# Where the modulation vector of a two-layer decoder trunk is summed: TensorE or VectorE

## The reference, cut to what matters

```
mod = silu(c) @ ada_w[layer] + ada_b[layer]      # 6 x 1024 numbers, one row for all tokens
h   = rms_norm(x, g_mix) * (1 + scale1) + shift1
proj = h @ w_in                                  # 2728 columns: SSD, MLA and MoBA inputs
y   = concat(ssd(...), mla(...), moba(...))      # each normalised
x   = x + gate1 * (y @ w_out)
h   = rms_norm(x, g_ffn) * (1 + scale2) + shift2
x   = x + gate2 * moe(h)                         # 16 experts, 2 of them for each token
```

## Time and profile before

| | us |
|---|---|
| median of 3 runs | 1639.8 (1638.78 to 1642.62) |
| profiled execution: its own time | 1642.98 |
| profiled execution: span, first to last instruction | 1641.2 |
| PE busy in the span | 1447.4 (88%) |
| DVE busy | 981.5 (60%) |
| ACT busy | 699.3 (43%) |
| DMA, mean rate | 226 GB/s |
| mean granted clock of TensorE | 0.930 of full speed |

### The profile page before, as it was taken

One profiled execution on the slowest core, in us unless ns is written; L12 is line 12 of the kernel. 1 busy time (PEld: TensorE's weight loads), 2 busy tenths in 40 slices (PEclk: granted clock), 3 DMA queues, 4 the chain that ended last, 5 costly groups with the idle time before them and its releaser, 6 DMA issues. The chain is left out here.

```text
span 1641.2 us, 16940 instructions
## 1 busy us (share of the span) xinstructions
PE 1447.4 (88%) x6459; PEld 1080.8 (66%) x6459; DVE 981.5 (60%) x1175; ACT 699.3 (43%) x945; POOL 137.1 (8%) x206
## 2 busy tenths in 40 slices
PE   8599988998859999999848999899796799999981
PEld 3388865676747777777426887747584677777761
DVE  0662055554559888888247412745457588888862
ACT  1423232463317666666014222226502566667640
POOL 0100013000101000100100000120000110001002
PEclk9699999988979999999978999899998799999995
DMA  8622342401549999997755227070117599999934
GB/s 336 228 93 69 128 183 103 154 1 52 234 169 357 402 398 399 406 395 285 280 193 199 89 68 260 1 253 4 52 37 322 205 388 398 398 398 406 396 138 167
DMA packets 90589, 371.08 MB, mean 226 GB/s; under 512 B 5241, under 2 KB 8039, under 8 KB 81160
## 3 DMA queue, kind: packets, MB, share of 16 engines
q1 hardware_dynamic: 75176, 313.30, 50.0%
q0 software_dynamic: 15328, 56.63, 8.9%
HBM read 336.09 MB, written 33.82 MB: 225 GB/s over the span
## 5 line engine op out<-in xcount | busy, mean ns | idle before, releaser
L971 PE MATMUL ps<-mod_rounded,work_rounded 128*128 128x512 f32 x340 | 140.1, 412 | 3.9 <-DVE work_rounded L1733 3.9
L973 PE MATMUL ps<-mod_rounded,work_rounded 128*128 128x512 f32 x340 | 135.7, 399 | 0.0
L1616 DVE TENSOR_TENSOR ring_rounded<-ring,mod_rounded 128x2048 fp32r<-128x2048 f32 (+1 forms) x54 | 102.6, 1930 | 32.7 <-ACT mod_rounded L1240 32.7
L687 PE MATMUL ps<-ring,csil 128*128 128x512 f32 x256 | 116.5, 615 | 0.0
L972 PE MATMUL ps<-ring_rounded,work_rounded 128*128 128x512 f32 x288 | 114.7, 398 | 0.0
L1616 DVE TENSOR_TENSOR work_rounded<-work,mod_rounded 128x2048 fp32r<-128x2048 f32 (+1 forms) x48 | 91.3, 1930 | 37.5 <-ACT mod_rounded L1240 37.5
L1106 ACT ACTIVATE work<-ps 128x512 f32<-128x512 f32 (+1 forms) x48 | 26.4, 551 | 187.9 <-PE ps L732 119.1
L972 PE MATMUL ps<-work_rounded 128*128 128x512 f32 x256 | 101.3, 396 | 0.0
L732 PE MATMUL ps<-ring_rounded,actT_rounded 128*128 128x512 f32 (+1 forms) x256 | 93.5, 365 | 0.0
L687 PEld LDWEIGHTS ps<-ring,csil 128*128 128x128 f32 x256 | 50.1, 198 | 61.5 <-issue 61.4
L1060 ACT ACTIVATE work<-x 128x1024 f32<-128x1024 f32 x16 | 16.9, 1058 | 171.0 <-DVE x L1326 82.2
(11 more groups left out here) (321 smaller groups left out, 3440.2 us busy)
## 6 DMA issues: line engine op xcount, KB each, us to landing
ring<-in_ada_w SPq DMA_DIRECT2D x22, 2048.0 KB, 8.4
ring<-in_moe_w_gate SPq DMA_DIRECT2D x18, 2048.0 KB, 10.4
ring<-in_moe_w_up SPq DMA_DIRECT2D x18, 2048.0 KB, 11.1
ring<-in_moe_w_down SPq DMA_DIRECT2D x18, 2048.0 KB, 11.5
work<-in_moe_w_gate SPq DMA_DIRECT2D x16, 2048.0 KB, 10.7
work<-in_moe_w_up SPq DMA_DIRECT2D x16, 2048.0 KB, 11.5
work<-in_moe_w_down SPq DMA_DIRECT2D x16, 2048.0 KB, 12.0
ring<-in_w_in SPq DMA_DIRECT2D x10, 2048.0 KB, 9.5
```

The lines of the kernel that those rows point to most:

```text
L687: mm = pe.matmul(ps[n % 2][:, :], csil[:, k:k + 1].to_broadcast([P, P]), w[:, k, :], start=k == 0, stop=k == KD - 1)
L971: pe.matmul(ps[j][:, :], xl, hi, start=k == 0, stop=False)
L973: mm = pe.matmul(ps[j][:, :], xh, hi, start=False, stop=k == KD - 1)
L1616: v.tensor_tensor(slots_r[3 * odd + j][:, 512 * k0:512 * k1], slots[3 * odd + j][:, 512 * k0:512 * k1], buf.bitcast(F32), ALU.subtract).th ...
```

## The change

1. PE no longer does the sums of the blocks inside the layers. A block becomes, on DVE, one product of the first 128x512 slice of weights with its column of silu(c), seven multiply-adds into a 128x512 accumulator, and an addition of the bias into one row. Then PE does one matmul with a matrix of ones (it sums over the partitions), ACT copies one row out, and every fourth block POOL stores four rows into a tensor in HBM (`store_ada_rows`). SP loads that tensor back, repeated over 128 partitions, into `mod`.
2. Twelve blocks run in each layer: blocks 4 to 11 in the input product (m = 0 to 7) and blocks 0 to 3 of the next layer in attention (m = 8 to 11, one or two of the 36 DVE operations for each n from 4 on). Nothing of it is left after the product, between SSD and attention, after attention, in the routing or at the end of layer 0. Layer 1 also sums four blocks, for which there is no use.
3. The weights of the modulation come in pieces of 1 MB into three buffers, in attention two. The input weights use two ring slots instead of three, and their later four loads are issued from ACT's queue, each after the last result of the block before has been copied out.
4. MoBA's heads come first. Their squares and norms are worked out ahead of SSD; MLA's squares go to n = 2, 5, 7 of attention, its head norms to ACT at n = 8, the scaling of the SSD output to n = 10 to 17.
5. The exponential, logarithm and squares of the latents on ACT move into the input product; the zeroing of spare rows by POOL moves into SSD; norm_ffn_g is loaded after attention.

```diff
+    ADA_AFTER = {4: 0, 8: 1, 12: 2, 13: 3, 14: 4, 16: 5, 18: 6, 20: 7}
+    ADA_LATE = {14: 8, 22: 9, 30: 10}
+    ADA_ADDS = KD + 1
+    HEADS = [4, 5, 6, 7, 0, 1, 2, 3]
...
             @block.tensor
-                def ada(b):
-                    n = group_no[("ada", b, 0)]
-                    w = slot_of("ada", b).rearrange("p (k n) -> p k n", k=KD)
-                    bank_free(n)
-                    for k in range(KD):
-                        mm = pe.matmul(ps[n % 2][:, :], csil[:, k:k + 1].to_broadcast([P, P]), w[:, k, :],
-                                       start=k == 0, stop=k == KD - 1)
...
+                def ada_total(m, bank):
+                    pe.wait_ge(*ada_total_ready(m))
+                    if m >= 2:
+                        pe.wait_ge(ada_row, m - 1)
+                    pe.matmul(bank[:, :], ones, ada_acc[m % 2], start=True, stop=True).then_inc(ada_ps, 1)
...
                         mm.then_inc(acc_ps, 1)
-                ada(4)
-                ada(5)
+                        if n in ADA_AFTER:
+                            ada_total(ADA_AFTER[n], ps[6 + ADA_AFTER[n] % 2])
...
                 pe.wait_ge(h_dn, 3)
-                for b in range(6, 10):
-                    ada(b)
                 pe.wait_ge(qkv_ev, 2 * T)
...
+                    if n in ADA_LATE:
+                        pe.wait_ge(q_sb, min(n // T + 2, 8))
+                        ada_total(ADA_LATE[n], ps[0])
                 pv(8 * T - 1)
...
-                with pe.If(L < DEPTH - 1):
-                    pe.wait_ge(hid_dn, NTL)
-                    pe.wait_ge(xt_ev, 2 * NTL)
-                    first_ada_sums(pe, ADA_AT_END, (5, 0, 1, 2))
...
             @block.scalar
+                def ada_row_out(m, bank):
+                    a.wait_ge(ada_ps, m + 1)
+                    p0 = 32 * (m % 4)
+                    a.activation(ada_row_of(m), bank[p0:p0 + 1, :], ACT.Copy).then_inc(ada_row, 1)
...
+                        if t == T - 1 and i + 2 < len(IN_ORDER):
+                            load_in(a, i + 2)
                         if 1 <= m <= 8:
                             conv_silu(m - 1)
                         m += 1
-                    if i + 2 < len(IN_ORDER):
-                        in_weights_hi(i + 2)
+                        if n in ADA_AFTER:
+                            ada_row_out(ADA_AFTER[n], ps[6 + ADA_AFTER[n] % 2])
+                        if t == 0 and 1 <= i < len(IN_ORDER) - 1:
+                            in_weights_hi(i + 1)
+                        if n == 15:
+                            dt_exp()
+                            latent_squares()
+                        if n == 18:
+                            a.wait_ge(sp_y, 1)
+                            a.activation(lny, y1, ACT.Ln).then_inc(sp_l, 1)
...
+                a.wait_ge(hss, 1)
+                heads_rstd(32, HP)
...
+                    if n == 8:
+                        a.wait_ge(hss, 2)
+                        heads_rstd(0, DQ)
...
             @block.vector
+                    w = buf[:, 512 * (k % 4):512 * (k % 4) + 512]
+                    if k:
+                        add(v.scalar_tensor_tensor(acc, w, csil[:, k:k + 1], acc, ALU.mult, ALU.add))
+                    else:
+                        if m >= 2:
+                            v.wait_ge(ada_ps, m - 1)
+                        add(v.tensor_scalar(acc, w, csil[:, 0:1], None, ALU.mult))
...
+                conv(0)
+                conv(1)
+                ada_sum(0)
+                conv(2)
+                conv(3)
+                conv(4)
+                in_weights_lo(2)
+                ada_sum(1)
+                conv(5)
+                conv(6)
+                conv(7)
+                in_weights_lo(3)
+                ada_sum(2)
+                ada_sum(3)
+                ada_sum(4)
                 in_weights_lo(4)
...
+                    if n in (2, 5, 7):
+                        mla_squares((2, 5, 7).index(n))
+                    if n == 10:
+                        v.wait_ge(yrs, 1)
+                    if 10 <= n < 18:
+                        y_norm((n - 10) // 2, (n - 10) % 2)
                     if n in (26, 30):
                         out_weights_lo(0, (n - 26) // 4)
+                    for q in range(max(n - 4, 0) * 9 // 7, max(n - 3, 0) * 9 // 7):
+                        ada_add(NEARLY + q // ADA_ADDS, q % ADA_ADDS)
                 head_out(7)
-                ada_out(10)
```

More of the change, by code:

```diff
@@ L285, in trunk @@
     next_ev = sem("next_ada_block_out")
+    ada_ld = [sem(f"ada_piece{j}_loaded") for j in range(3)]
+    ada_late_ld = [sem(f"ada_late_piece{j}_loaded") for j in range(2)]
+    ada_b_ld = sem("ada_bias_rows_loaded")
+    ada_late_b_ld = sem("ada_late_bias_rows_loaded")
+    ada_sm = sem("ada_products_added")
+    ada_ps = sem("ada_row_in_psum")
+    ada_row = sem("ada_row_out")
+    row_st = [sem(f"ada_rows_stored{j}") for j in range(3)]
     modb_ld = sem("mod_bias_loaded")
@@ L543, in trunk @@
     y_col = [0, 128, 256, 384, CQ0, CQ0 + 128, MQ0, MQ0 + 128]
-    base_ld = [16 * (last_load[j] // 3 + 2) + (16 if (load_no[("mla", 0)] + 1) % 3 == j else 0) for j in range(3)]
+    base_ld = [32 + 16, 64 + 16, 64 + 16]
     def expert_loaded(e, odd, j):
@@ L594, in _ @@
                     sp.dma_start(hpar[:, n, :], A[name][bass.ds(L, 1)].broadcast_to([P, NH])).then_inc(par, 16)
[L595 to L610 removed]
+                load_in(sp, 1)
@@ new lines, in _ @@
+                load_ada_bias(0, ada_b_ld)
+                load_ada_bias(1, ada_b_ld)
+                for m in range(NEARLY):
+                    for half in range(2):
+                        piece = 2 * m + half
+                        if piece == 2:
+                            sp.wait_ge(h_ps, 2 * T)
+                        if piece >= 3:
+                            sp.wait_ge(*ada_added((piece - 3) // 2, (piece - 3) % 2))
+                        load_ada(m, half)
+                sp.wait_ge(*ada_added(NEARLY - 1, 1))
@@ new lines, in _ @@
+                sp.wait_ge(zero_wr, 16)
+                load_ada_bias(2, ada_late_b_ld)
+                sp.wait_ge(qkv_ps, 2 * T)
+                load_ada(NEARLY, 0)
+                load_ada(NEARLY, 1)
+                sp.wait_ge(kr_dn, 1)
+                sp.wait_ge(hss, 2)
+                load_out(1)
+                for m in range(NEARLY + 1, NADA):
+                    for half in range(2):
+                        sp.wait_ge(*ada_added(m - 1, half))
+                        load_ada(m, half)
@@ L1379, in _, with conv @@
                 v.wait_ge(pads, 2)
-                for f in range(8):
+                def conv(f):
                     v.wait_ge(win_ev, f + 1)
```

371 lines of the change are left out of this document (199 added, 172 removed).

## The result

The changed kernel takes **1627.8 us** (median of 5 runs, 1624.4 to 1630.3); the kernel before took 1639.8 beside it. The ratio is 0.9924, 95% interval 0.9906 to 0.9942: faster by 12.0 us where 25.5 were forecast. The time is inside the range given (1586 to 1642) and at the very edge of the likeliest case's own (1600 to 1628), but the gain is under half of the one forecast. The profiled execution of after is 1627.81 (span 1626.1), that of before 1642.98: 15.2 apart.

The account below looks back on a forecast made before the run. PE, busy 88% of the span, was taken as the bound. A, B, D, F, C and E gave -6.1 a layer, twice -12.2; with G -25.5: 1642.98 to 1617.5, or 1614 us as a median; range 1586 to 1642.

Parts of the forecast that it names:

- the likeliest case: Whole kernel: the forecast itself, 1614 us with its own range 1600 to 1628, chance 0.55.
- A: Input product: eight ones-matmuls added to a PE without gaps, 6.9 us, plus 1.7 of waits; +8.6 a layer, upper end +18.
- B: Last product to first SSD work on DVE: blocks 4 and 5 go, latents normed earlier; -15.3 a layer, between -13.9 and -17.5.
- C: MLA's projections to first turned head: MoBA's first head already staged, only the last copy's 0.7 us remains; -28.8 a layer.
- D: Attention: additions, squares, scalings and waits lengthen heads by 26.6, slower clock adds 4; +31 a layer, between +12 and +52.
- E: Behind attention: block 10 gone, but the norm still waits for POOL; -2.1 a layer.
- F: Routing: block 11 gone, DVE loses 0.7, PE comes back cold; +0.5 a layer, between -0.7 and +2.
- G: End of layer 0: last store to last combination shrinks from 38.5 us to layer 1's 25.2; -13.3, once.
- the wait for the root: Attention, n = 9: staging the first MLA head waits for ACT's logarithm and exponential, two table loads included; 2.0 us.
- Rival 2: Attention: PE waiting for DVE stays at 1.2 GHz and becomes the bound; D +52, whole kernel 1656 us; chance 0.12.
- Rival 3: Input product: weight blocks from ACT's queue collide with 16 MB of pieces; A +18, whole kernel 1633 us; chance 0.12.

Follow-up runs that it names:

- warm_tiles: Changed kernel plus unused 512-column PE products before the turn of the probabilities at tiles 0, 1 and 2 of attention heads, none at tile 3; 1612.9 us (0.9839).
- even_heads: Changed kernel with next heads turned two tiles earlier, MLA squares in seven pieces, their root on POOL, first MLA scaling later, additions spread over n = 4 to 31; 1589.2 us.
- sp_loads: Changed kernel with the input weights of blocks 2 to 5 issued by SP again, between the modulation pieces, instead of by ACT; 1631.6 us (0.9946).

## Why the prediction was right in the mechanism and wrong in the size

Step by step, us, layers 0 and 1:

| step | forecast | measured |
|---|---|---|
| A, product | +8.6 each | +9.5, +11.6 |
| B, product to SSD | -15.3 each | -15.3, -15.5 |
| C, SSD to attention | -28.8 each | -28.9, -28.9 |
| D, attention | +31 each | **+34.2, +37.3** |
| E, behind attention to the ranks | -2.1 each | -2.1, -2.6 |
| F, routing | +0.5 each | +2.06, +2.06 |
| G, end of layer 0 | -13.3 | -13.6 |
| what no step named | 0 | -5.0 |

- **B, C and G** hold to a few tenths. Each was a count of records on a path that waited for nothing else, and what is late next was read from rows.
- **D is the term that was mis-sized.** Its larger part, DVE's order, holds: without the growth of the wait, attention grew by 26.8 and 27.9 us against the 26.6 foreseen (25.6 of them "work" of the six heads), the wait for the root is 2.1 against 2.0, and an add cost 0.73 against 0.746. The smaller part is the step that failed: "for a quarter of eight heads that is +4". Its price for a head was near, 2.0 us against the 2.2 between a wait at 0.50 (5.25) and the 3.09 of before. Its share of the heads was wrong. In layer 0 four of the six waits stood at 0.50 and took 5.1 to 5.7 us; the fourth, with 0.89 in its middle, took 3.92, and only the last stood at 1.00 (3.12). In layer 1 all six took 4.8 to 5.7 us, at 0.50 to 0.75 in their middle. The wait grew by 7.4 and 9.4 us instead of 4, and warm_tiles took 4.0 and 4.2 of it back with products that compute nothing. About half of attention stood at 1.2 GHz. Together D is 9.5 us over for both layers.
- Rival 2 was the right fear at the wrong size. I argued against it "that a PE which becomes the bound is busy again". The rows of even_heads show PE busy 20 of 20 us at 0.50; being the bound did not end it there. TensorE: Matmul & The Clock Gate, "What's actually happening", in the Trainium skill has activity release the full rate; the trace agrees in so far as unused products held it at 1.00, and does not in those 20 us. In the changed kernel itself the clock returned in parts of most heads, so attention did not become 118 us; why it returned there and not in those 20 us is not shown.
- **A** is 3.9 us over for both layers. Its size was near for layer 0 (waits of 3.0 us where 1.7 were foreseen; 3.7 in layer 1). Part of layer 1's excess may be no part of the change: the same product takes from 132.6 to 136.9 us. Rival 3 is out: no weight block came late, and sp_loads shows that the queue does not matter.
- **E** came out at -2.1 in layer 0 partly by luck. The norm starts there only 1.2 us earlier behind attention than before (7.3 us instead of 8.5): ACT now copies out the last total, 0.59 us, ahead of the squares, which start 0.9 us later than they did. The other 0.9 come after the norm. In layer 1 the norm starts 2.4 us earlier.
- **F** was put at +0.5 with "PE comes back cold" and an upper end of +2; it was +2.06. Block 11 cost nothing where it stood and held the clock for the ranks. The upper end was the right value: the first 20 of the ranks' 28 records take 4.45 us instead of 2.41; the last eight, for the counts, take 0.37 and 0.35.
- Of the -5.0 that no step named, 1.7 lie in the start-up ahead of layer 0. The rest are differences of 0.1 to 2.0 us of both signs, most of them in stages that the change leaves alone; they stay unexplained.

Together: 9.5 for D, 3.9 for A, 3.1 for F, less 6.2 for B, C, E, G and what no step named: 10.3 us of the forecast gain that did not come. That 6.2 us came back there is luck, as no step foresaw 5.0 of them. The two profiled executions are 15.2 us apart, the medians 12.0; the profiled one of before was 3.2 over its median and that of after was on it.

## What to carry to other kernels

When work moves from a full engine to one with idle time, ask of each idle microsecond whether it stands before or after the chain that closes the loop: here moving 23 additions from one side of the fourth tile to the other took 14.7 us out of the heads' work and put 6.1 and 4.1 into their waits, and sending the chain's first link two tiles earlier was worth twice the whole change. Then price what the relieved engine does when it idles: on PE that is the clock, for the work that stays as well as for the next stage, and one row of granted clock per head shows it. An edit that "costs nothing because it lies beside other work" may itself have been what held the clock.

## What the runs showed of the hardware

- 33 unused products of 512 columns per layer made attention 5.2 and 5.6 us shorter, with its granted clock going from 0.73 and 0.72 to 1.00 and 0.98; the kernel went from 1627.8 to 1612.9. The same idea with a product inside the critical wait gained nothing (1626.8).
- The granted clock stayed at 0.50 for 20 us in which PE is shown busy throughout (69 matmuls, many of them transposes), some 4 us after a stretch of 4 us with 2.8 us busy (1047 to 1051). The ends of matmuls in these records are modelled, so how busy the array was in that time stays open.
- A multiply-add with both sources f32 in SBUF is 748 ns at 512 columns in attention and 750 over the whole run (134 of them), 9% over a two-source addition (690). The half throughput of the page weighed in the prediction (Vector Engine (DVE) Microarchitecture Reference, "Points that are easy to get wrong", in the Trainium skill) is not in these rows either.
- POOL's power -0.5 on 128x16 took 2.9 and 3.4 us beside DVE's work, about 0.2 us per column, but off ACT's queue it cost DVE 1.2 us of waiting instead of the 4.4 behind ACT's two table loads.
